# One attention head between half tiles, short divisors, projections by operand halves, an early first weight tile

## The chip, the cores and the metric

The kernel runs on one core of a Trainium2 chip. The metric is the device time of one execution in microseconds (us). TensorE (PE in the profile, PEld for its weight loads) does all matrix products, VectorE (DVE), ScalarE (ACT) and GpSimd (POOL) the rest, and SyncE (SP) issues the DMAs. The engines run their own instruction lists in order and meet at semaphores, which the program sets and waits for by hand.

## What is computed

Two blocks in a row on 256 tokens of width 1024: a gated delta-rule mixer, a forgetting attention, then a sliding-window attention beside a multiscale pooling, a merge, an output projection, and a dense evaluation of a routed expert layer with 16384 experts. The change touches the entrance of the first mixer and the middle of the second block:

```python
h = rmsnorm(x, norm_w[i]) * (1 + scale) + shift          # scale, shift from cond @ ada_w
proj = h @ w_in                                          # q k v z, then 16 columns b and 16 columns a
beta = sigmoid(b);  g = -exp(A_log) * softplus(a + dt_bias)
...
z = rmsnorm_2(h, ln_mix_g) @ w_in_2 + b_in_2             # 15 tiles of 256 columns: C_ORDER
q, k, v, pz, ga, gp = split(z)
y_a = sliding_window_attention(q, k, v, sinks) @ w_attn_up
cnt = minimum(t1, w);  pooled = (cj - lag) / cnt - pf    # windows w = 2, 4, 8, 16, t1 = 1..256
y_p = multiscale_pool(pz) @ w_pool_up
merged = sigmoid(ga) * y_a + sigmoid(gp) * y_p
h = h + merged @ w_o
```

## The kernel before

**Weight tiles.** Every large product runs over tiles of 1024 by 256 weights. A tile is loaded by one 1 MB DMA into one of four RAW slots (`load`), split by ACT into a rounded high part WHI (`hi`, L628 to L635) and by DVE into the rest WLO (`lo`, L1117 to L1121), each with two slots, and PE then makes three products for each of eight chunks of the operand: high by high, low by high, high by low. `columns_half` (L1803 to L1815) makes one half of the output columns' rows of a tile in 24 matmuls, `columns_tile` both halves in 48, `tokens_tile` (L1824 to L1835) the same number with the operand as the stationary side. The operand itself is split the same way: ACT writes XHI (`split_half`, L642), DVE XLO (`split_x`, L1131, and `split_low`, L1483), each in two halves of four chunks, and `x_halves` makes PE wait for a half when it comes to it (`x_split`). `tile_done` says that PE has finished a tile: `hi` waits for it before it overwrites the slot, two tiles on, and the eviction of the output bank waits for it too. `bank_free` says that one of the two output banks is evicted. Tiles are numbered through the whole program; T_AIN, T_CIN, T_PUP, T_AUP and T_WO are the first numbers of the first mixer's entrance, the second block's entrance, the pooling's up projection, the attention's up projection and the output projection.

**The beginning.** PE makes eight 256-column products of the modulation (L1861) while DVE turns each result into columns of MC by a product with the identity and a sum (L1188, L1190, loop n = 0 to 7). `norm(0)` on PE transposes x. When the eighth sum is there, DVE makes the scale and the shift (`modulation`), ACT writes H and XHI (L673, L642), DVE writes XLO. PE then multiplies H by the 32 columns of b and a (TWA, L1871, 16 matmuls that are two pieces each in the profile), and only then comes the first tile of T_AIN. `hi` and `lo` of that tile stand behind `norm(0)` on ACT and behind `split_x(0, H)` on DVE.

**The second block's entrance.** ACT evicts tile n of T_CIN with its bias (`project`, L937), and `hi` of tile n + 1 stands ahead of it. DVE has `lo` of the tiles one after another, with small work between the first ones: the divisors INV, first the smaller of t1 and w, then the reciprocal of all 256 columns for each of four windows (L1524, L1528), then four copies of v (L1533). POOL waits for these reciprocals (`inv_ready`) and makes the pooled sums, of which PE needs the last behind tile 8. Behind tile 11, whose columns are the first four heads' queries, PE has the logits of the first head (`logits(8)`, L2096 and L2097), then the whole tile 12. DVE has `lo` of tiles 4 to 13, then `queries_c(0)` (L1450, which the logits wait for), then `softmax(8)` (L1462 to L1479). ACT has `hi` of tile 13, the eviction of tile 12, and then the exponents (`exponents(8)`, L870). In eight rounds, one for a pair of heads, PE then transposes the probabilities (`turn`, L2106), makes the next logits, a half tile (or a tile with four chunks), and applies the probabilities to v (`apply`, L2116, L2117).

**The projections.** The attention's output feeds T_AUP (four tiles). DVE multiplies each result by its gate (L1572) and adds it to MG (L1574). When all four are added (`mg_done` 4) ACT splits MG (L642), DVE follows (L1131), and T_WO, four tiles by `tokens_tile`, starts with its first half.

## Time and profile before

| | us |
|---|---|
| median of 3 runs | 1847.93 |
| lowest, highest | 1843.86, 1848.80 |
| the profiled execution | 1848.02 |
| its span in the trace | 1846.3 |
| PE busy | 1708.7 (93%) |
| DVE, ACT, POOL busy | 1194.2, 900.3, 356.5 |

PE is busy for 93% of the span, but a busy PE is not always at full speed: the granted clock has two levels, 1.00 (2.4 GHz) and 0.50 (1.2 GHz), and it was 0.972 in the mean. So two things are to be read: where PE waits and for whom, and for how long the clock stands at 0.50 behind such a wait. In rows of the timeline the first number is the start in us from the beginning of the span, the second the duration, `xN` the number of merged instructions, and the bracket the idle time of the engine before the row with what ended it.

### The profile page before, as it was taken

How to read it: one execution, taken by the hardware profiler on the slowest of the kernel's cores; microseconds unless marked ns; L12 is line 12 of the kernel's file. 1: busy time of each engine (PE TensorE's matmuls, PEld its weight loads, DVE VectorE, ACT ScalarE, POOL GpSimd, SP SyncE). 2: the span in 40 equal slices, each digit the busy share in tenths (PEclk: the TensorE clock that was granted, in tenths of full speed). 3: DMA queues.
4: the chain of work that ended last, by engine and by line, in shares of the span. 5: the costliest groups of instructions: out<-in, count | busy, mean ns of one | idle time of the engine just before them, and what ended most of it. 6: DMA issues, size and time to landing. Idle time of an engine off the chain costs nothing.

```text
span 1846.3 us, 35420 instructions
## 1 busy us (share of the span) xinstructions
PE 1708.7 (93%) x11788; PEld 1572.8 (85%) x11788; DVE 1194.2 (65%) x2403; ACT 900.3 (49%) x1611; POOL 356.5 (19%) x225
## 2 busy tenths in 40 slices
PE   7899989999899986989889899999999989999998
PEld 6799788888799876988879899999999968888887
DVE  2686377776445655537633899968999865555554
ACT  1665523332335554445433344467777755555554
POOL 2000000000000000400000677776666420000000
PEclk9999999999899998999989899999999999999999
DMA  9555301010734333431553455555444356666664
GB/s 278 173 184 182 123 24 47 23 45 24 251 114 138 115 103 97 137 126 63 154 123 83 136 164 166 165 169 155 141 141 138 103 150 193 193 193 194 192 193 136
DMA packets 210746, 255.24 MB, mean 138 GB/s; under 512 B 14871, under 2 KB 192763, under 8 KB 210683
## 3 DMA queue, kind: packets, MB, share of 16 engines
q1 hardware_dynamic: 210683, 254.39, 45.6%
q8 instruction: 41, 0.67, 0.2%
q14 instruction: 22, 0.18, 0.0%
HBM read 253.29 MB, written 1.05 MB: 138 GB/s over the span
## 4 chain that ended last, share of the span: by engine, by line
PE 63%; issue 19%; POOL 8%; DVE 5%; ACT 3%; DMA 1%; SPq 1%; DVEq 0%; POOLq 0%; ACTq 0%
PE ps L2273 19%; PE ps L1815 13%; PE ps L2224 8%; POOL w_lo L618 7%; PE ps L2056 3%; PE ps L2249 3%; PE ps L1965 2%; PE ps L1954 2%; PE ps L1966 2%; PE ps L1861 2%; PE ps L1944 1%; PE ps L1835 1%; PE ps L1886 1%; PE ps L1905 1%; DMA raw<-in_u_experts 1%
## 5 line engine op out<-in xcount | busy, mean ns | idle before, releaser
L618 POOL TENSOR_TENSOR w_lo<-raw,w_hi 128x1024 fp32r<-128x1024 f32 x128 | 307.1, 2400 | 366.1 <-ACT w_hi L1009 365.5
L1815 PE MATMUL ps<-x_hi,w_hi 128*128 128x256 f32 x1104 | 319.8, 290 | 8.8 <-DVE w_lo L1121 5.7
L2224 PE MATMUL ps<-x_hi,w_hi 128*128 128x256 f32 x1024 | 297.4, 290 | 20.3 <-ACT arena L1014 12.4
L1815 PE MATMUL ps<-x_lo,w_hi 128*128 128x256 f32 x1104 | 315.4, 286 | 0.0
L1815 PE MATMUL ps<-x_hi,w_lo 128*128 128x256 f32 x1104 | 315.2, 286 | 0.0
L2224 PE MATMUL ps<-x_lo,w_hi 128*128 128x256 f32 x1024 | 290.7, 284 | 0.0
L2224 PE MATMUL ps<-x_hi,w_lo 128*128 128x256 f32 x1024 | 290.6, 284 | 0.0
L1779 DVE TENSOR_TENSOR w_lo<-raw,w_hi 128x1024 fp32r<-128x1024 f32 x124 | 152.0, 1226 | 143.8 <-ACT w_hi L1099 143.8
L1815 PEld LDWEIGHTS ps<-x_hi,w_hi 128*128 128x128 f32 x1104 | 215.1, 195 | 12.7 <-DVE w_lo L1121 6.4
L2224 PEld LDWEIGHTS ps<-x_hi,w_hi 128*128 128x128 f32 x1024 | 197.2, 193 | 24.6 <-issue 17.7
L1099 ACT ACTIVATE w_hi<-raw 128x1024 fp32r<-128x1024 f32 x124 | 131.6, 1061 | 172.9 <-PE ps L2273 172.9
L1815 PEld LDWEIGHTS ps<-x_lo,w_hi 128*128 128x128 f32 x1104 | 215.1, 195 | 0.5 <-issue 0.5
L1815 PEld LDWEIGHTS ps<-x_hi,w_lo 128*128 128x128 f32 x1104 | 214.9, 195 | 0.0
L2224 PEld LDWEIGHTS ps<-x_lo,w_hi 128*128 128x128 f32 x1024 | 197.5, 193 | 0.0
L2224 PEld LDWEIGHTS ps<-x_hi,w_lo 128*128 128x128 f32 x1024 | 197.2, 193 | 0.0
L1009 ACT ACTIVATE w_hi<-raw 128x1024 fp32r<-128x1024 f32 x128 | 134.8, 1053 | 123.9 <-DVE raw L1603 123.7
L1603 DVE STREAM_TRANSPOSE raw<-raw 128x1024 f32<-128x1024 f32 x128 | 158.4, 1238 | 22.2 <-DMA raw<-in_u_experts 17.0
L1121 DVE TENSOR_TENSOR w_lo<-arena,w_hi 128x2048 fp32r<-128x2048 f32 (+1 forms) x43 | 96.8, 2251 | 101.9 <-ACT w_hi L635 101.9
L2273 PE MATMUL ps<-w_hi,x_hi 128*128 128x512 f32 x512 | 158.7, 391 | 4.0 <-DVE x_lo L1774 4.0
L2273 PE MATMUL ps<-w_hi,x_lo 128*128 128x512 f32 x512 | 158.4, 391 | 0.0
L2273 PE MATMUL ps<-w_lo,x_hi 128*128 128x512 f32 x512 | 158.3, 390 | 0.0
L1121 DVE TENSOR_TENSOR w_lo<-raw,w_hi 128x2048 fp32r<-128x2048 f32 (+1 forms) x44 | 99.1, 2255 | 74.7 <-ACT w_hi L635 74.6
(336 smaller groups left out, 3235.3 us busy)
## 6 DMA issues: line engine op xcount, KB each, us to landing
raw<-in_u_experts SPq DMA_DIRECT2D x512, 128.0 KB, 2.5
raw<-in_v_experts SPq DMA_DIRECT2D x128, 512.0 KB, 4.3
arena<-in_ada_w SPq DMA_DIRECT2D x20, 1024.0 KB, 5.2
raw<-in_a_w_in SPq DMA_DIRECT2D x12, 1024.0 KB, 5.3
arena<-in_a_w_in SPq DMA_DIRECT2D x12, 1024.0 KB, 5.3
raw<-in_b_w_in SPq DMA_DIRECT2D x8, 1024.0 KB, 5.7
arena<-in_b_w_in SPq DMA_DIRECT2D x8, 1024.0 KB, 5.8
raw<-in_w_in SPq DMA_DIRECT2D x8, 1024.0 KB, 5.4
```

What stands on the lines that cost most here:

```text
L618: pool.tensor_tensor(UTL[e], UT[e % 2], UTH[e].bitcast(F32), ALU.subtract).then_inc(utl_ready, 1)
L1009: act.activation(UTH[e % 4], UT[e % 2], ACT.Copy).then_inc(uth_ready, 1)
L1099: act.activation(VH[u], VRAW[u], ACT.Copy).then_inc(high_ready, 1)
L1121: v.tensor_tensor(WLO[:, slot, 0:k, :], RAW[raw_slot(base, u)][:, 0:k, :], WHI[:, slot, 0:k, :].bitcast(F32), ALU.subtract).then_inc(lo_re ...
L1603: v.transpose(UT[s_].rearrange("p (k a j) -> p a k j", k=KC, a=4), URAW[s_].rearrange("p (a k i) -> p a k i", a=4, k=KC)).then_inc(ut_read ...
L1779: v.tensor_tensor(VL[u], VRAW[u], VH[u].bitcast(F32), ALU.subtract).then_inc(low_ready, 1)
L1815: ins = mm(o[:, b * S:b * S + S], w[:, slot, kk, b * P:b * P + P], xx[:, (kk + turn) % KC, :], start=(kk == 0 and n == 0), stop=(kk == k - ...
L1861: ins = mm(ps[u % 2][:, 0:TW], CONDR[:, kk, :], RAW[u][:, kk, :], start=(kk == 0), stop=(kk == KC - 1))
L2056: ins = mm(o, xx[:, kk, t * P:t * P + P], w[:, slot, kk, :], start=(kh == 0 and u % 2 == 0 and kk == 0 and n == 0), stop=(kh == 1 and kk = ...
L2224: ins = mm(ps[e % 2][:, 0:S], w[e % 4][:, kk * P:kk * P + P], xx[:, kk, :], start=(kk == 0 and n == 0), stop=(kk == KC - 1 and n == 2))
L2249: ins = mm(GB.rearrange("p (e t) -> p t e", t=4)[:, q, :], OHJ[:, c % 2, q, :], OHI[:, c % 2, q, :], start=True, stop=True, skip_group_che ...
L2273: ins = mm(ps[4 + 2 * t + h][:, :], g[:, u, t * P:t * P + P], w[u][:, 512 * h:512 * h + 512], start=False, stop=False, skip_group_check=True)
```

## The change

1. **First head among half tiles.** PE makes the first half of tile 12, the first head's logits, then the second half. DVE's `lo` of tile 13 moves behind `softmax(8)`, so that `queries_c(0)` follows `lo` of tile 12. ACT's eviction of tile 12 moves behind `exponents(8)`.
2. **Short divisors.** INV is filled with the constant 1/w by a memset, and the reciprocal is taken of the first w columns alone: 2, 4, 8 and 16 columns.
3. **Projections by operand halves.** The last T_AUP tile first makes chunks 4 to 7 for both output halves and signals `up_half`; ACT and DVE then split the first two merged tiles into chunks 4 to 7 of XHI and XLO while PE makes chunks 0 to 3. The first T_WO tile uses these chunks 4 to 7 first, for both token tiles, and chunks 0 to 3, with the last two merged tiles, after them. The other T_WO tiles take the chunks in the same turned order.
4. **The first T_AIN tile early.** `hi` of the tile stands behind ACT's `statistics(0)` and ahead of its wait for the modulation, `lo` ahead of the eighth pass of DVE's loop. PE has the tile ahead of the product for b and a. `hi` and `lo` of the third tile stand ahead of the tail. The product for b and a is one with 48 columns (b in 0 to 15, a in 32 to 47, the second layer's f weights between them) in place of two with 16, 8 matmuls in place of 16. For that TWA is loaded by two DMAs with rows of 64 B in place of one with 128 B, `rows_in` counts seven.

```diff
-            sp.dma_start(TWA, a_w_in[0, :, 6144:6176].rearrange("(k p) n -> p k n", p=P)).then_inc(rows_in, 16)
+            for g in range(2):
+                sp.dma_start(TWA[:, :, 32 * g:32 * g + 16],
+                             a_w_in[0, :, 6144 + 16 * g:6160 + 16 * g].rearrange("(k p) n -> p k n", p=P)).then_inc(rows_in, 16)
...
@@ scalar
                 statistics(r, eps)
+                if r == 0:
+                    hi(T_AIN, 0, 0)
...
-            for n in range(13):
+            for n in range(12):
                 hi(T_CIN, 0, n + 1)
                 project(n)
...
             act.wait_ge(c_pos, 4)
+            hi(T_CIN, 0, 13)
             exponents(8)
+            project(12)
...
+            act.wait_ge(mg_done, 2)
+            act.wait_ge(up_half, 1)
+            act.activation(XHI[:, 4:8, :], MG[:, 0:4, :], ACT.Copy).then_inc(xhi_ready, 1)
             act.wait_ge(mg_done, 4)
-            split_x(8, MG, 75)
+            act.wait_ge(tile_done, 75 + 2)
+            act.activation(XHI[:, 0:4, :], MG[:, 4:8, :], ACT.Copy).then_inc(xhi_ready, 1)
...
@@ vector
             for n in range(8):
+                if n == 7:
+                    lo(T_AIN, 0, 0)
                 v.wait_ge(raw_free, 4 + n + 1)
...
-                v.tensor_scalar(INV[:, j, :], T1, float(2 << j), None, ALU.min).then_inc(c_prep, 1)
+                v.memset(INV[:, j, :], 1.0 / (2 << j)).then_inc(c_prep, 1)
...
-                v.reciprocal(INV[:, j, :], INV[:, j, :]).then_inc(inv_ready, 1)
+                v.reciprocal(INV[:, j, 0:2 << j], T1[:, 0:2 << j]).then_inc(inv_ready, 1)
...
-            for n in range(4, 14):
+            for n in range(4, 13):
                 lo(T_CIN, 0, n)
             queries_c(0)
             softmax(8)
+            lo(T_CIN, 0, 13)
             queries_c(1)
...
                 lo(T_AUP, 0, u + 1)
+                if u == 3:
+                    split_low(8, 0, slice(4, 8), MG[:, 0:4, :])
                 product(T_AUP, 0, u)
...
@@ tensor
             norm(0)
-            pe.wait_ge(rows_in, 16 * 6)
+            x_round[0] = 0
+            columns_tile(T_AIN, 0, 0)
+            pe.wait_ge(rows_in, 16 * 7)
...
-            for j in range(2):
-                for kk in range(KC):
-                    ins = mm(ps[2][0:16, j * 256:j * 256 + 256], TWA[:, kk, 16 * j:16 * j + 16], H[:, kk, :],
-                             start=(kk == 0), stop=(kk == KC - 1))
+            for kk in range(KC):
+                ins = mm(ps[2][0:48, 0:256], TWA[:, kk, :], H[:, kk, :], start=(kk == 0), stop=(kk == KC - 1))
...
-                elif n == 11:
-                    pe.wait_ge(c_k, 1)
-                    pe.wait_ge(c_pos, 4)
-                    logits(8, cK[:, 0:S])
+            columns_half(T_CIN, 0, 12, 0)
+            pe.wait_ge(c_k, 1)
+            pe.wait_ge(c_pos, 4)
+            logits(8, cK[:, 0:S])
+            columns_half(T_CIN, 0, 12, 1)
...
+            for half in range(2):
+                pe.wait_ge(x_split, 17 + half)
+                for t in range(TT):
+                    for kk in range(4 * half, 4 * half + 4):
+                        for n, (xx, w) in enumerate(((XHI, WHI), (XLO, WHI), (XHI, WLO))):
+                            ins = mm(bank(T_WO, 0)[:, t * TW:t * TW + TW], xx[:, (kk + 4) % KC, t * P:t * P + P], w[:, slot, kk, :],
+                                     start=(kk == 0 and t == 0 and n == 0), stop=(kk == KC - 1 and n == 2), skip_group_check=True)
```

**The beginning, on DVE.** Before, with the two last passes of the modulation's loop (output banks ps0 and ps1), the scale and shift, the operand's low halves and the first two weight tiles' low parts:

```order
L1188 TENSOR_TENSOR arena<-ps0,small 128x256
L1190 TENSOR_REDUCE small<-arena 128x2
L1188 TENSOR_TENSOR arena<-ps1,small 128x256
L1190 TENSOR_REDUCE small<-arena 128x2
L1179 TENSOR_TENSOR small<-small 128x8
L1180 SCALAR_TENSOR_TENSOR small<-small 128x8
L1182 TENSOR_TENSOR small<-small 128x8
L1131 TENSOR_TENSOR x_lo<-arena,x_hi 128x1024 x2
L1121 TENSOR_TENSOR w_lo<-raw01,w_hi 128x2048 x2
```

The same place in the changed kernel:

```order
L1202 TENSOR_TENSOR arena<-ps0,small 128x256
L1204 TENSOR_REDUCE small<-arena 128x2
L1133 TENSOR_TENSOR w_lo<-raw01,w_hi 128x2048
L1202 TENSOR_TENSOR arena<-ps1,small 128x256
L1204 TENSOR_REDUCE small<-arena 128x2
L1191 TENSOR_TENSOR small<-small 128x8
L1192 SCALAR_TENSOR_TENSOR small<-small 128x8
L1194 TENSOR_TENSOR small<-small 128x8
L1143 TENSOR_TENSOR x_lo<-arena,x_hi 128x1024 x2
L1133 TENSOR_TENSOR w_lo<-raw01,w_hi 128x2048
L1133 TENSOR_TENSOR w_lo<-arena,w_hi 128x2048
```

The first tile's low part now stands ahead of the loop's last pass, and the third tile's low part, which reads the arena, has come up behind the second's.

**The second attention's beginning, on PE.** Before, the last matmuls of tile 11 (ps1), the first head's logits with their masks (ps2, ps4), and the first of tile 12 (ps0):

```order
L1815 MATMUL ps1<-x_hi,w_lo 128x256
L2096 MATMUL ps2<-arena 128x128
L2097 MATMUL ps2<-small 128x128
L2096 MATMUL ps2<-arena 128x256
L2097 MATMUL ps2<-small 128x256
L2096 MATMUL ps4<-arena 128x128
L2097 MATMUL ps4<-small 128x128
L2096 MATMUL ps4<-arena 128x256
L2097 MATMUL ps4<-small 128x256
L1815 MATMUL ps0<-x_hi,w_hi 128x256
```

In the changed kernel the rows on both sides of the logits are of tile 12:

```order
L1838 MATMUL ps0<-x_lo,w_hi 128x256
L1838 MATMUL ps0<-x_hi,w_lo 128x256
L2119 MATMUL ps2<-arena 128x128
L2120 MATMUL ps2<-small 128x128
L2119 MATMUL ps2<-arena 128x256
L2120 MATMUL ps2<-small 128x256
L2119 MATMUL ps4<-arena 128x128
L2120 MATMUL ps4<-small 128x128
L2119 MATMUL ps4<-arena 128x256
L2120 MATMUL ps4<-small 128x256
L1838 MATMUL ps0<-x_hi,w_hi 128x256
```

A half tile of 24 matmuls now stands between the end of tile 11 and the logits.

**From the last T_AUP tile to the first T_WO tile, on DVE.** Before, with the last two gated results (ps1, ps0) and the operand's low halves:

```order
L1572 TENSOR_TENSOR arena<-ps1,arena 128x512
L1574 TENSOR_TENSOR arena<-arena 128x512
L1121 TENSOR_TENSOR w_lo<-arena,w_hi 128x2048
L1572 TENSOR_TENSOR arena<-ps0,arena 128x512
L1574 TENSOR_TENSOR arena<-arena 128x512
L1131 TENSOR_TENSOR x_lo<-arena,x_hi 128x1024 x2
L1121 TENSOR_TENSOR w_lo<-raw01,w_hi 128x2048
L1157 TENSOR_TENSOR arena<-arena,ps1 128x2x256
```

The same place in the changed kernel:

```order
L1595 TENSOR_TENSOR arena<-ps1,arena 128x512
L1597 TENSOR_TENSOR arena<-arena 128x512
L1133 TENSOR_TENSOR w_lo<-arena,w_hi 128x2048
L1503 TENSOR_TENSOR x_lo<-arena,x_hi 128x1024
L1595 TENSOR_TENSOR arena<-ps0,arena 128x512
L1597 TENSOR_TENSOR arena<-arena 128x512
L1503 TENSOR_TENSOR x_lo<-arena,x_hi 128x1024
L1133 TENSOR_TENSOR w_lo<-raw01,w_hi 128x2048
L1169 TENSOR_TENSOR arena<-arena,ps1 128x2x256
```

One of the two operand halves has moved ahead of the last gated result.

## Rows read from the trace of the kernel before

**Rows 1.** Timeline, beginning; start, duration, engine, line, names, count, idle before

```profile
44.79 0.42 DVE L1188 TENSOR_TENSOR arena<-ps,small 128x256 f32<-128x256 f32 x1 [2.58 <-PE ps L1861]
49.24 1.23 DVE L1131 TENSOR_TENSOR x_lo<-arena,x_hi 128x1024 fp32r<-128x1024 f32 x1 [3.09 <-ACT x_hi L642]
52.15 1.23 DVE L1131 TENSOR_TENSOR x_lo<-arena,x_hi 128x1024 fp32r<-128x1024 f32 x1 [1.69 <-ACT x_hi L642]
...
51.18 0.58 PE L1867 MATMUL ps<-small 1*128 1x16 f32 x2 [4.67 <-ACT arena L673]
51.68 9.71 PE L1871 MATMUL ps<-arena,small 128*16 128x256 f32 x32
...
65.36 0.51 ACT L702 ACTIVATE arena<-arena,small 16x256 f32<-16x256 f32 x1
```

**Rows 2.** DMA: the first T_AIN tile's issue at 34.50, us to landing

```profile
raw<-in_a_w_in SPq DMA_DIRECT2D x1, 1024.0 KB, 6.7
```

**Rows 3.** DMA packets from 35.5 to 36.0 us, mostly TWA's

```profile
DMA packets 843, 0.11 MB, mean 211 GB/s; under 512 B 833, under 2 KB 843, under 8 KB 843
```

**Rows 4.** Windows: busy of PE, PEld, DVE, ACT, POOL, then PEclk, DMA share, GB/s

```profile
57.00:57.50 0.50, 0.50 (x3) 0.19 (x2) 0.50 (x1) 0.00 (x0) 0.00 (x0) 0.95 0.00 0
```

**Rows 5.** Timeline, ACT and DVE, around tile 4 of T_CIN

```profile
759.14 1.91 ACT L635 ACTIVATE w_hi<-raw 128x2048 fp32r<-128x2048 f32 x1
...
764.17 0.84 ACT L937 ACTIVATE arena<-ps,small 128x256 f32<-128x256 f32 x2 [1.82 <-PE ps L1815]
...
774.38 0.84 ACT L937 ACTIVATE arena<-ps,small 128x256 f32<-128x256 f32 x2 [7.58 <-PE ps L1815]
...
757.14 6.58 DVE L1528 RECIPROCAL arena<-arena 128x256 f32<-128x256 f32 x4
764.37 5.14 DVE L1121 TENSOR_TENSOR w_lo<-raw,w_hi 128x2048 fp32r<-128x2048 f32 x2
```

**Rows 6.** Timeline, ACT, DVE and PE, tile 11 to the second head's transposes

```profile
817.43 0.84 ACT L937 ACTIVATE arena<-ps,small 128x256 f32<-128x256 f32 x2 [2.71 <-PE ps L1815]
...
820.10 2.29 DVE L1121 TENSOR_TENSOR w_lo<-raw,w_hi 128x2048 fp32r<-128x2048 f32 x1 [3.05 <-ACT w_hi L635]
822.31 0.61 DVE L1450 TENSOR_SCALAR arena<-arena,small 128x256 f32<-128x256 f32 x2
...
823.07 0.77 PE L2096 MATMUL ps<-arena 128*128 128x128 f32 x2 [5.67 <-DVE arena L1450]
...
836.34 1.80 PE L2106 MATMUL ps<-small,arena 128*128 128x128 f32 x6 [2.99 <-DVE arena L1479]
...
844.56 0.60 PE L2116 MATMUL ps<-arena 128*128 128x256 f32 x2
...
845.87 0.82 PE L2106 MATMUL ps<-small,arena 128*128 128x128 f32 x6
```

**Rows 7.** Timeline, PE, first and last piece of a later head's logits

```profile
880.23 0.39 PE L2096 MATMUL ps<-arena 128*128 128x128 f32 x2
...
881.87 0.27 PE L2097 MATMUL ps<-small 128*128 128x256 bf16 x1
```

**Rows 8.** Timeline, DVE, first and last step of a later head's softmax

```profile
854.20 0.62 DVE L1462 TENSOR_REDUCE small<-ps 128x1 f32<-128x128 f32 x2 [1.11 <-PE ps L2097]
...
857.75 0.55 DVE L1479 TENSOR_SCALAR arena<-arena,small 128x128 f32<-128x128 f32 x2
```

**Rows 9.** Windows of PE: busy, granted clock, DMA share, GB/s

```profile
835.00:836.00 1.00, 0.00 (x0) 0.65 0.00 0
```

**Rows 10.** Timeline, DVE, last T_AUP tile and first T_WO tiles

```profile
917.74 0.69 DVE L1572 TENSOR_TENSOR arena<-ps,arena 128x512 f32<-128x512 f32 x1 [1.46 <-PE ps L1815]
...
920.35 2.36 DVE L1131 TENSOR_TENSOR x_lo<-arena,x_hi 128x1024 fp32r<-128x1024 f32 x2 [1.19 <-ACT x_hi L642]
...
930.27 0.69 DVE L1157 TENSOR_TENSOR arena<-arena,ps 128x512 f32<-128x512 f32 x1 [4.96 <-PE ps L1835]
...
936.03 0.69 DVE L1157 TENSOR_TENSOR arena<-arena,ps 128x512 f32<-128x512 f32 x1 [1.46 <-PE ps L1835]
```

86 lines of the change are left out of this document (54 added, 32 removed).

## The prediction

> **What bounds the kernel now.** I read the waits of TensorE first. It is busy nearly throughout, so a microsecond taken from any other engine counts only where PE waits for it. Then I read the timeline around each long wait, to see which instruction ended it and what stood ahead of that instruction in its queue, and last the windows with the granted clock, because behind each long wait the clock stands at 0.50 for some microseconds and PE's own work takes twice as long. The change addresses four places. (a) At the beginning PE idles 4.67 us for the normed input and then spends 9.71 us on the product for b and a, of which the first 5.4 us are at half clock: the clock was back at 57.05 [rows 1, 4]. (b) Tile 4 of the second block's entrance: the evictions of tiles 3 and 4 start 10.21 us apart, against 5.76 between two tiles that wait for nothing [rows 5, 10]. (c) The first head of the second attention: PE idles 5.67 us for its queries and 2.99 us for its softmax [rows 6]. (d) Between the last up tile and the first output tile the evictions are 12.53 us apart, again against 5.76 [rows 10].
>
> A tile of 48 matmuls is 5.76 us at full clock, 0.12 a matmul, a half tile 2.88, and at half clock the double is an upper bound. All four gains lie on PE's path, and what follows each is timed from PE's progress (weight loads wait for `lo_ready`, which moves along), so I add them and take nothing off further down.
>
> **(b) Short divisors.** The four reciprocals of 256 columns take 6.58 us, and `lo` of tile 4 stands behind them: it starts at 764.37, though its high part was there at 759.14 + 1.91 = 761.05, and tile 3 is done at 764.13 [rows 5]. With 2 to 16 columns, 30 in place of 1024, the four cost a fraction of that; even at 1 us together the copies are done before 761.05, `lo` runs from there to about 763.4 (763.7 at the 2.57 that it takes beside POOL), and PE waits for nothing. The memsets take the place of four instructions of like size, with more than 1 us of slack behind them. What goes is the wait of 2.7 us and the half clock that it caused: 10.21 - 5.76 = **4.45 us**. POOL gets its divisors earlier too; its results are needed only behind tile 8. If `lo` of tile 4 came late by a POOL operation, 0.5 us of this would be lost: 3.9 to 4.5.
>
> **(c) The first head.** Times are those of the old trace. Tile 11 is done at 817.38. PE goes on with the first half of tile 12, whose low part is ready, to 820.3. DVE has nothing ahead of the queries but the eviction of tile 11 (817.43 + 0.84), so they are ready at 818.9, and the logits start at 820.3 with no wait. At full clock they take 1.76 us, from 880.23 to 0.12 behind 881.87 [rows 7]. Second half of tile 12 to 824.9. The softmax of a head takes 4.1 us from its first reduction to its last product (854.20 to 858.30) [rows 8]; it starts 1.1 us into the logits, at 821.4, and ends at 825.5, so the wait of 2.99 us becomes one of about 0.6, and the six transposes end at 826.1. Now the new wait: `lo` of tile 13 (2.2) and the next queries (0.6) stand behind the softmax on DVE, and the next logits need the queries: 825.5 + 2.8 = 828.3. PE waits 2.2 us; nobody but PE waits for that. Then logits 1.76, a half tile 2.88 and the application 1.31 (844.56 to 845.87 [rows 6]) give 834.3 for the next transposes, which stood at 845.87: 11.6 us. I take off 0.7, an estimate: ACT's and DVE's split of tile 14 (1.9 and 2.3) now comes later against PE than before and delays the third head's reductions.
>
> How the clock takes the new wait is open. It was granted full until 0.3 us into the window from 835 to 836 (0.65 in its mean), so it fell about 2 us into the wait that had begun at 833.35 [rows 6, 9]; The new wait of 2.2 us with 0.6 just ahead of it is near that one, so I assume that it falls, and comes back within 3.5 to 6 us of work. That costs half of 3.4 at the least, 3 at the most, and some is covered by the softmax: I take 1.6. Term: 11.6 - 0.7 - 1.6 = **9.3 us**; ends 7.5 and 11.6.
>
> **(d) Operand halves.** The first merged half (chunks 4 to 7) can be split when the last up tile, which runs from 911.94 to 917.70, is half done, at 914.8. `hi` (1.9) and `lo` (2.3) of the output tile follow the tile before and keep DVE until 916.3; with 1.23 for the operand's low part it ends at 917.5, just ahead of the last up tile's end at 917.70. So the output tile starts there, without the wait for 921.7. Its first 24 matmuls end at 920.6. The second half is ready as the old first one was, 920.35 + 1.23 = 921.6 [rows 10]. PE waits 1.1 us and ends the tile at 921.7 + 2.9 = 924.6, against 930.23 before. Next late would be `lo` of the second output tile: ACT splits it from 920.2 to 922.1, DVE from 922.2 to 924.5, a tie. Term: **5.6 us**, with 4.5 if the tie is lost and 6.0 as the upper end.
>
> **(a) The early tile.** The first tile lands 6.7 us after its issue at 34.50, so at 41.2 [rows 2]. Ahead of it in the queue there are now 1024 more rows of 64 B. 833 such small packets went in half a microsecond [rows 3], so 1024 take 0.6, and with the issue I take 0.7: landing 41.9. ACT's high part (1.92) is ready at 43.8, DVE's low part (2.25) at 46.1, and the loop's last product, which ran at 44.79, stands behind it: everything from there to XLO is 1.3 us later. That wait is the price of this part, and ACT, PE and all behind them pay it. The ends are 0.6 (no slower landing at all) and 2.5 (packets twice as slow).
>
> The Trainium skill's page DMA: Bandwidth & Descriptors, section Why small descriptors are slow, says a packet costs a cycle per 32 B and about 3 more. By it two rows of 64 B cost 10 cycles where one of 128 B costs 7, so TWA would add not 0.6 but about 0.26 us, and this term would be 0.4 larger. In the trace the packet rate hardly depended on the size (833 of mostly 128 B in one half microsecond), so I keep 0.7.
>
> PE then starts the tile at 50.6 + 1.3 = 51.9, at half clock. Its first 12 matmuls (0.24 at most, 0.214 as the pieces of the old row show) end at 54.5, the second operand half is there at 53.5 + 1.3 = 54.8. As before the clock returns 5.9 us after the restart, at 57.8: 14 matmuls by then, 22 more at 0.12: done at 60.5. The product for b and a has 16 pieces in place of 32; the old ones took 0.22 each once the clock was back, so 3.5, with the sinks' 0.2 it ends at 64.2. The second tile ends at 70.0. Before, two tiles followed 61.39 and ended at 72.9. Term: **2.9 us**, ends 1.5 and 4.3. The evacuation of the first bank stands behind ACT's tail, which took 4.5 us (61.39 to 65.87 [rows 1]) and takes until 68.7, with the bank's copy 69.3: 0.7 ahead of need.
>
> **Sum.** 2.9 + 4.45 + 9.3 + 5.6 = 22.25 us. The profiled execution took 1848.02, 0.1 above the median, so the forecast is 1848.02 - 22.25 = 1825.8 us. The runs of before spread by 5 us, which the range has to hold too.
>
> **Rivals.**
>
> *The clock holds in (c), or the softmax runs beside more.* For it: the wait is shorter than the one behind which the clock is seen to fall [rows 9]. It gives 1.6 to 2.3 us more, and with the upper ends of (a) and (d) 1820 to 1821.
>
> *The early tile costs what it brings.* DVE's low part in the loop holds back the whole norm. If the tile lands after 43.5, the loss there is over 3 us and (a) brings about 1: 1828; with (d)'s tie lost too 1829 to 1830. Against it: nothing else of size is in the DMA queue ahead of the tile.
>
> *(c) brings half.* If the second head's chain (exponents, `lo` of tile 13, queries) is longer than the rows say by the eviction of tile 12, which ACT now does between, and the clock is low through two rounds, the term is 5: 1830.
>
> *The other side: the clock does not come back in the attention.* A later round has some 6.7 us of PE work at full clock (0.7 + 1.76 + 2.88 + 1.31). If the new wait of 2.2 us let the clock fall and each following softmax wait kept it low, seven rounds would take up to 6.7 us more each, 47 in all, less the 22: 1873. It decides at whether PE is kept busy through the round behind the wait. Before, it was, after a longer idle time: by 845.87 the six transposes took 0.82 us, where behind the wait they took 1.80 [rows 6]. The Trainium skill's page TensorE: Matmul & The Clock Gate, section HAM oscillation, describes such a loop, whose bursts are short against its waits and which runs at the low clock in every round. In the rounds here the transposes of the next head follow the application at once (845.87, with no idle time [rows 6]), so the trace so far speaks against it.
>
> *It does not do what it says.* That would be so if PE found the halves unready everywhere: the order shows each moved instruction in its place, so this is left to single terms.
>
> **How the numbers follow.** The forecast case, all four terms within their ends, 1821.5 to 1829: 0.76. More than that, under 1821.5: 0.09. Early tile or first head worth half, 1829 to 1835: 0.11. Between 1835 and 1842.4: 0.02. The clock stays low, or another mishap that leaves no gain: 0.02. A measurement of this kernel can tell about 0.3%, 5.5 us, from no change. Faster by more than that (under 1842.4) is then 0.98, within it 0.01, slower 0.01. The range 1820 to 1831.5 leaves out some 0.05 below and 0.1 above.
>
> **What would show it.** (b): evictions of tiles 3 and 4 are 5.8 us apart, and no wait for `w_lo` there. (c): no wait ahead of the first logits, one of about 2.2 us ahead of the second, and the time from the eviction of tile 11 to the second head's transposes is 17 to 19 us, where it was 28.4. (d): a wait of about 1.1 us in the middle of the first output tile, and evictions 6.9 us apart, where they were 12.5. (a): DVE's last product of the loop 1.3 us later than 44.79, the second tile done at about 70. I would be wrong if the clock were low for longer than 7 us at a time anywhere in the attention, or if a new wait stood behind these places on another engine.

## The result, and the profile after

The changed kernel takes 1821.32 us (median of 6 runs, 1816.2 to 1824.96) where the kernel before took 1845.71 beside it (6 runs, 1843.1 to 1848.8): ratio 0.9866, with a 95% interval from 0.9844 to 0.9889. The forecast was 1825.8 in 1820 to 1831.5, so the median lies inside the range, 4.5 us under the forecast and just below the forecast case (1821.5 to 1829, chance 0.76), in the stretch that was given 0.09. It is no run's time: three runs lie at 1816.2 to 1818.64 and three at 1823.99 to 1824.96. The profiled execution took 1823.99 (span 1822.1), 24.0 less than the profiled one of before, where the sum said 22.25. One of the ten runs of the operand halves alone, below, took 2825.75 us at a mean granted clock of 0.556 and is left out of its median and ratio.

All places are read between the same two landmarks in both traces:

| place and landmarks, us | before | after | gain | forecast |
|---|---|---|---|---|
| (a) second T_AIN tile done (ACT's next high part) | 73.20 | 70.27 | 2.93 | 2.9 |
| (b) evictions of tiles 3 and 4 apart | 10.21 | 5.80 | 4.41 | 4.45 |
| (c) eviction of tile 11 to the second head's transposes | 28.44 | 19.57 | 8.87 | 10.0 |
| from these transposes to the last T_AUP eviction | 71.87 | 71.84 | 0.03 | -0.7 |
| (d) last T_AUP eviction to first T_WO eviction | 12.53 | 7.07 | 5.46 | 5.6 |
| from the second T_AIN tile to the eviction of tile 3 | 690.97 | 689.18 | 1.8 | 0 |
| from the fourth T_WO eviction to the end | 898.75 | 898.05 | 0.7 | 0 |

The forecast's 9.3 for (c) is 11.6 less 1.6 for the clock, which lie between these landmarks, and less 0.7, which lies behind them.

**The beginning** (timeline of after: start us, duration us, engine, line, names, count, idle before; it answers to [rows 1]):

```profile
41.41 0.43 DVE L1202 TENSOR_TENSOR arena<-ps,small 128x256 f32<-128x256 f32 x1 [2.57 <-PE ps L1884]
...
41.86 1.91 ACT L638 ACTIVATE w_hi<-raw 128x2048 fp32r<-128x2048 f32 x1 [24.61 <-DMA raw<-in_a_w_in]
...
43.80 2.29 DVE L1133 TENSOR_TENSOR w_lo<-raw,w_hi 128x2048 fp32r<-128x2048 f32 x1 [1.51 <-ACT w_hi L638]
46.01 0.42 DVE L1202 TENSOR_TENSOR arena<-ps,small 128x256 f32<-128x256 f32 x1
...
50.44 1.22 DVE L1143 TENSOR_TENSOR x_lo<-arena,x_hi 128x1024 fp32r<-128x1024 f32 x1 [3.08 <-ACT x_hi L645]
...
60.56 3.65 PE L1894 MATMUL ps<-arena,small 128*48 128x256 f32 x16
...
70.27 1.92 ACT L638 ACTIVATE w_hi<-arena 128x2048 fp32r<-128x2048 f32 x1 [0.17 <-PE ps L1838]
```

The same two landmarks before, the loop's seventh product and ACT's high part behind the second tile:

```profile
41.34 0.42 DVE L1188 TENSOR_TENSOR arena<-ps,small 128x256 f32<-128x256 f32 x1 [2.58 <-PE ps L1861]
...
73.20 1.92 ACT L635 ACTIVATE w_hi<-arena 128x2048 fp32r<-128x2048 f32 x1 [2.42 <-PE ps L1815]
```

The tile lands at 41.86 (41.9 was said), DVE's low part ends as the loop's last product starts, at 46.01 (46.1), and that product is 1.2 later than before. The price is plain to see: the first operand half starts at 50.44, where it stood at 49.24.

**Tile 4 of the second block** (timeline of after, DVE and ACT; it answers to [rows 5]):

```profile
752.43 0.44 DVE L1548 RECIPROCAL arena<-arena 128x2 f32<-128x2 f32 x4
...
756.37 2.78 DVE L1133 TENSOR_TENSOR w_lo<-raw,w_hi 128x2048 fp32r<-128x2048 f32 x1 [2.77 <-ACT w_hi L638]
...
759.45 0.84 ACT L943 ACTIVATE arena<-ps,small 128x256 f32<-128x256 f32 x2 [1.82 <-PE ps L1838]
...
765.25 0.84 ACT L943 ACTIVATE arena<-ps,small 128x256 f32<-128x256 f32 x2 [3.16 <-PE ps L1838]
```

The four reciprocals take 0.44 us together where they took 6.58. DVE now idles 2.77 us ahead of the low part and waits for ACT's high part; before, the high part was there and the low part stood behind the reciprocals.

**The first head** (timeline of after, ACT, DVE and PE; it answers to [rows 6]):

```profile
808.30 0.84 ACT L943 ACTIVATE arena<-ps,small 128x256 f32<-128x256 f32 x2 [2.71 <-PE ps L1838]
...
815.59 0.55 DVE L1499 TENSOR_SCALAR arena<-arena,small 128x128 f32<-128x128 f32 x2
816.06 2.28 DVE L1133 TENSOR_TENSOR w_lo<-raw,w_hi 128x2048 fp32r<-128x2048 f32 x1
818.26 0.61 DVE L1470 TENSOR_SCALAR arena<-arena,small 128x256 f32<-128x256 f32 x2
...
810.98 0.39 PE L2119 MATMUL ps<-arena 128*128 128x128 f32 x2
...
815.60 1.14 PE L2129 MATMUL ps<-small,arena 128*128 128x128 f32 x6
...
818.92 0.79 PE L2119 MATMUL ps<-arena 128*128 128x128 f32 x2 [2.18 <-DVE arena L1470]
...
827.87 0.82 PE L2129 MATMUL ps<-small,arena 128*128 128x128 f32 x6
```

The first logits (810.98) wait for nothing. The new wait stands where it was forecast, ahead of the second head's logits, and is 2.18 us long: softmax, then `lo` of tile 13, then the queries. The windows of after there (us; busy of PE, PEld, DVE, ACT, POOL; granted clock; DMA) show the clock go to its half level, 1.2 GHz, within that wait and come back 6.8 us of half clock later:

```profile
818.00:819.00 1.00, 0.08 (x1) 0.08 (x1) 0.87 (x3) 0.00 (x0) 0.00 (x0) 0.68 0.00 0
...
825.00:826.00 1.00, 1.00 (x10) 1.00 (x9) 0.93 (x5) 1.00 (x1) 0.00 (x0) 0.90 0.00 0
```

**Up and out projection** (timeline of after, DVE and PE, then its window; it answers to [rows 10]):

```profile
899.71 0.69 DVE L1595 TENSOR_TENSOR arena<-ps,arena 128x512 f32<-128x512 f32 x1 [0.32 <-PE ps L2211]
...
902.32 1.23 DVE L1503 TENSOR_TENSOR x_lo<-arena,x_hi 128x1024 fp32r<-128x1024 f32 x1 [1.20 <-ACT x_hi L994]
...
906.78 0.69 DVE L1169 TENSOR_TENSOR arena<-arena,ps 128x512 f32<-128x512 f32 x1 [0.44 <-PE ps L2222]
...
903.60 0.39 PE L2222 MATMUL ps<-w_hi,x_hi 128*128 128x256 f32 x1 [0.96 <-DVE x_lo L1503]
```

```profile
900.00:904.00 4.00, 3.04 (x25) 2.83 (x25) 2.31 (x3) 2.85 (x2) 0.00 (x0) 1.00 1.11 230
```

One wait of 0.96 in the middle of the tile (1.1 was said), at full clock throughout.

**What the sum did not have.** Between (a) and (b) no numbered part of the change removes work or a wait, and yet 1.8 us went there. The wait at the second block's entrance is the same to the hundredth; before, then after:

```profile
731.82 3.67 PE L1843 MATMUL ps<-small,arena 128*128 128x128 f32 x16 [11.30 <-DVE arena L1142]
```

```profile
728.68 3.67 PE L1866 MATMUL ps<-small,arena 128*128 128x128 f32 x16 [11.30 <-DVE arena L1154]
```

What differs is how long the clock is low around it: the windows of before show 0.52 over 21 us, those of after 0.55 over 14 us and then 0.95:

```profile
722.00:743.00 21.00, 9.52 (x43) 9.15 (x44) 9.13 (x8) 12.43 (x23) 0.74 (x2) 0.52 0.20 64
```

```profile
718.00:732.00 14.00, 3.32 (x16) 3.27 (x16) 4.70 (x6) 7.49 (x17) 0.74 (x2) 0.55 0.29 94
732.00:743.00 11.00, 8.55 (x68) 8.02 (x67) 5.92 (x7) 6.83 (x10) 0.00 (x0) 0.95 0.22 70
```

Adding up (1 - granted clock) x 2 x width over windows of 2 us gives 20.5 us at half clock there before and 13.7 after, and over the whole span 102.7 before and 78.7 after. All times at half clock below are worked out so. Of the 24 us fewer, 3.4 lie behind the wait of (b), 6.8 at (c), 6.8 at (d) and 6.8 at this entrance.

The other traces bear this place out. The wait is 11.29 or 11.30 in all 14. The stretch from the second T_AIN tile to the eviction of tile 3 takes 690.8 to 691.0 us in the three with 20.5 us at half clock at the entrance (before, c_head_alone, three_moves) and 689.0 to 689.5 in the nine with 13.7, whether the change is in them or not.

The 0.7 behind the output projection is another matter: there both traces have the same half clock (10.2, 10.2 and 6.8 us at three places, and the clock low from about 4 us before the end). Six traces with this pattern take 897.8 to 898.8 us for that stretch, so 0.7 is inside what that stretch varies by, and its cause is open.

### The profile page after: what moved, and what is told of

It reads as the page before. It is cut to its first block, busy times and chain, and to the rows that moved or that the text cites. A ratio compares the mean times of both kernels' runs of the same rounds, so it can differ in the third digit from the quotient of the medians.

```text
span 1822.1 us, 35333 instructions
## 1 busy us (share of the span) xinstructions
PE 1696.4 (93%) x11772; PEld 1565.1 (86%) x11772; DVE 1187.0 (65%) x2403; ACT 900.1 (49%) x1611; POOL 357.0 (20%) x225
## 4 chain that ended last, share of the span: by engine, by line
PE 63%; issue 19%; POOL 8%; DVE 5%; ACT 3%; DMA 1%; SPq 1%; DVEq 0%; POOLq 0%; ACTq 0%
PE ps L2318 19%; PE ps L1838 13%; PE ps L2269 9%; POOL w_lo L621 7%; PE ps L2079 3%; PE ps L2294 3%; PE ps L1988 2%; PE ps L1977 2%; PE ps L1989 2%; PE ps L1967 2%; PE ps L1858 1%; PE ps L1909 1%; PE ps L1884 1%; PE ps L1928 1%; PE ps L2119 1%
## 5 line engine op out<-in xcount | busy, mean ns | idle before, releaser
L2269 PE MATMUL ps<-x_hi,w_hi 128*128 128x256 f32 x1024 | 297.5, 291 | 19.7 <-ACT arena L1026 11.8
L1838 PEld LDWEIGHTS ps<-x_hi,w_hi 128*128 128x128 f32 x1088 | 211.0, 194 | 16.3 <-issue 9.1
L2269 PEld LDWEIGHTS ps<-x_hi,w_hi 128*128 128x128 f32 x1024 | 197.1, 192 | 24.1 <-issue 17.3
L1838 PEld LDWEIGHTS ps<-x_lo,w_hi 128*128 128x128 f32 x1088 | 211.1, 194 | 0.5 <-issue 0.5
L1838 PEld LDWEIGHTS ps<-x_hi,w_lo 128*128 128x128 f32 x1088 | 210.9, 194 | 0.0
L2269 PEld LDWEIGHTS ps<-x_lo,w_hi 128*128 128x128 f32 x1024 | 197.4, 193 | 0.0
L2269 PEld LDWEIGHTS ps<-x_hi,w_lo 128*128 128x128 f32 x1024 | 197.1, 193 | 0.0
```

Source lines behind the costliest of these rows:

```text
L1838: ins = mm(o[:, b * S:b * S + S], w[:, slot, kk, b * P:b * P + P], xx[:, (kk + turn) % KC, :], start=(kk == 0 and n == 0), stop=(kk == k - ...
L2269: ins = mm(ps[e % 2][:, 0:S], w[e % 4][:, kk * P:kk * P + P], xx[:, kk, :], start=(kk == 0 and n == 0), stop=(kk == KC - 1 and n == 2))
```

## Experiments

Each kernel is the one before with one part, or the changed one with one to three edits. "Beside it" is the kernel before in the same series.

### One part alone

Four kernels, each the one before with the lines of one numbered part of the change and nothing else: part 4 (T_AIN's `hi`, `lo` and `columns_tile` early, TWA by two DMAs, 48 columns), part 2, part 1 (tile 12 by halves around `logits(8)`, `lo` of tile 13 behind `softmax(8)`) and part 3 (`up_half`, chunks 4 to 7 first). Their diffs are pieces of the one shown; that of part 2 is

```diff
-                v.tensor_scalar(INV[:, j, :], T1, float(2 << j), None, ALU.min).then_inc(c_prep, 1)
+                v.memset(INV[:, j, :], 1.0 / (2 << j)).then_inc(c_prep, 1)
-                v.reciprocal(INV[:, j, :], INV[:, j, :]).then_inc(inv_ready, 1)
+                v.reciprocal(INV[:, j, 0:2 << j], T1[:, 0:2 << j]).then_inc(inv_ready, 1)
```

Part 4, the early tile. 

> The kernel before with the early first weight tile and the 48-column product alone. Theory: the terms stand at separate places and add, so this is worth what the landmark shows in the full change, 2.9 us (second tile done at about 70.3 us in place of 73.2), and the median falls by 3 us. A rival, that most of the full change's 24 us comes from PE's clock everywhere and not from the four places, expects a fall of more than 6 us or none here, with the mean granted clock moved.

Part 2, the divisors. 

> The kernel before with the short divisors alone. Theory of separate places: the evictions of tiles 3 and 4 of the second block's entrance are 5.8 us apart in place of 10.2, the median falls by 4.4 us, and the tiles behind show no new wait. The rival (clock everywhere) expects another sum than 4.4, by more than 3 us.

Part 1, the first head. 

> The kernel before with the first head between the two halves of tile 12 alone. Theory: from the eviction of tile 11 to the second head's transposes 19.6 us in place of 28.4, a fall of 8.9 us; the wait for the second head's queries is 2.2 us, and the clock falls behind it as in the full change. If the clock holds in this run (its fall depends on where the wait lies), 10.5 to 11 us.

Part 3, the operand halves. 

> The kernel before with the up and output projections by operand halves alone. Theory: the evictions of the last up tile and the first output tile are 7.1 us apart in place of 12.5, the clock stays at 1.00 through the wait of 1 us in the middle of the output tile, and the median falls by 5.5 us.

| part alone | median (range, runs), beside 1843.95 | ratio [95%] | at its own landmarks |
|---|---|---|---|
| (a) | 1839.79 (1837.67 to 1845.31, 10) | 0.9973 [0.9958, 0.9987] | loop's seventh product to second tile 28.56, was 31.86 |
| (b) | 1841.01 (1839.68 to 1845.53, 10) | 0.9983 [0.9971, 0.9994] | 5.82, was 10.21 |
| (c) | 1837.09 (1832.43 to 1838.6, 5) | 0.9948 [0.9927, 0.9969] | 18.32, was 28.44 |
| (d) | 1837.49 (1835.56 to 1841.59, 9) | 0.9961 [0.9947, 0.9974] | 7.07, was 12.53 |

The medians fall by 4.2, 2.9, 6.9 and 6.5, 20.4 together, and the whole change's by 20 (its second series, below) to 24 (its first). Expected were 3, 4.4, 8.9 and 5.5, so (b) and (c) fell short by 1.5 and 2, and (a) and (d) went beyond by about 1. Each interval is 2 to 4 us wide to either side, so the medians agree with parts that add but can't prove it. The rival of the first expectation (most of the 24 us is the clock everywhere, so that the early tile alone brings over 6 us or nothing, with its mean clock moved) isn't borne out: 4.2 us, at mean clocks of 0.972 to 0.977 as in the kernel before. The landmarks decide better: alone the parts gain 3.3, 4.4, 10.1 and 5.5 there, against 3.0, 4.4, 8.9 and 5.5 in the whole, so none is hidden behind another. In (c) alone the second wait has less half clock behind it (3.4 us instead of 6.8). For (a) the seventh product is the base, because the run of (a) alone is 0.5 us ahead before that landmark.

The trace of (d) alone holds a clean price for the old wait in (b), since that part is undone here and the clock happened to hold (timeline, then a window):

```profile
764.43 0.39 PE L1821 MATMUL ps<-x_hi,w_hi 128*128 128x256 f32 x1 [2.70 <-DVE w_lo L1125]
```

```profile
766.00:768.00 2.00, 2.00 (x19) 2.00 (x18) 1.11 (x1) 0.00 (x0) 2.00 (x3) 1.00 0.98 322
```

The evictions of tiles 3 and 4 are 8.73 apart there and 10.21 in before. So of (b)'s gain 2.9 (8.73 - 5.82) is the wait, and 1.5 is what the 3.4 us of half clock behind it cost.

### The two new waits taken away

On the changed kernel, the second head's queries ahead of the low part:

```diff
             softmax(8)
-            lo(T_CIN, 0, 13)
             queries_c(1)
+            lo(T_CIN, 0, 13)
```

> The changed kernel, with the second head's queries ahead of the low part of tile 13 on DVE. Theory: the wait of 2.2 us ahead of the second head's logits and the half clock behind it (from 818.7 to 825.1) are both of this order. With it turned, PE waits less than 0.5 us there, the clock stays at 1.00, PE then waits about 0.5 us for the low part of tile 13, and the second head's transposes start 4 to 5 us earlier than 827.87; 1 to 2 us of it are given back in the next round, where tile 14's split delays the third head's reductions. Net 3 us. Rival: the gap is not what lets the clock fall, or the softmax chain takes its place: less than 1 us.

Measured 1817.79 (1816.98 to 1818.06, 4 runs) beside 1843.96: 0.9848 [0.9828, 0.9868]. Its timeline, DVE then PE, and a window:

```profile
815.08 0.61 DVE L1470 TENSOR_SCALAR arena<-arena,small 128x256 f32<-128x256 f32 x2
815.61 2.28 DVE L1133 TENSOR_TENSOR w_lo<-raw,w_hi 128x2048 fp32r<-128x2048 f32 x1
...
815.75 0.49 PE L2119 MATMUL ps<-arena 128*128 128x128 f32 x2
...
822.22 0.82 PE L2129 MATMUL ps<-small,arena 128*128 128x128 f32 x6
```

```profile
817.00:818.00 1.00, 0.81 (x6) 0.40 (x4) 1.00 (x2) 0.00 (x0) 0.00 (x0) 1.00 0.00 0
```

The second logits follow the transposes with no idle time, and the clock stays full. From the eviction of tile 11 (807.32) to the second head's transposes it is 14.90, 4.67 less than in the changed kernel. A part is given back (1 to 2 us were expected): from there to the last T_AUP eviction it takes 72.45 where it took 71.84, because one later round takes 7.18 instead of 6.59. Net, from the eviction of tile 11 to the last T_AUP eviction, it is 87.35 against 91.41, 4.1 less (3 was expected).

The early tile's low part out of the loop:

```diff
             for n in range(8):
-                if n == 7:
-                    lo(T_AIN, 0, 0)
...
             modulation(0, MC[:, 0:8], MC[:, 8:16], 0)
+            lo(T_AIN, 0, 0)
             split_x(0, H)
```

> The changed kernel, with the first weight tile's low part behind the scale and shift on DVE, ahead of the operand's low half. Theory: the prediction's price of 1.3 us for the early tile is DVE's low part in the loop. DVE is idle for 3.1 us behind the modulation, and the low part takes 2.3, so the loop's last product is back at about 44.8, everything behind it 1.2 us earlier than in the changed kernel, second tile done at about 69.1. Rival (the norm is late for another reason, the DMA or ACT): no gain.

Measured 1821.64 (1821.47 to 1824.71, 4 runs), 0.9875 [0.9853, 0.9897]. In its trace the eighth product follows the seventh by 3.46, in the changed kernel by 4.60, so the low part inside the loop costs 1.1:

```profile
40.31 0.42 DVE L1200 TENSOR_TENSOR arena<-ps,small 128x256 f32<-128x256 f32 x1 [2.57 <-PE ps L1883]
...
43.77 0.42 DVE L1200 TENSOR_TENSOR arena<-ps,small 128x256 f32<-128x256 f32 x1 [2.58 <-PE ps L1883]
...
45.04 2.29 DVE L1133 TENSOR_TENSOR w_lo<-raw,w_hi 128x2048 fp32r<-128x2048 f32 x1
```

From the seventh product to the second tile's end it is 27.74 here and 28.86 in the changed kernel. The expected 1.2 is met, and the rival of no gain is out. The median doesn't show that 1.1: its trace has 17.1 us at half clock behind the T_WO tiles where the changed kernel's has 10.2, and 2.4 us more from the fourth T_WO eviction to the end. It tells something else too. The wait of (c) is in it, 2.18 us as before, and the clock held:

```profile
816.80 0.49 PE L2118 MATMUL ps<-arena 128*128 128x128 f32 x2 [2.18 <-DVE arena L1469]
```

```profile
816.00:817.00 1.00, 0.20 (x1) 0.20 (x2) 0.75 (x3) 0.00 (x0) 0.00 (x0) 1.00 0.00 0
```

Landmark to landmark it is 16.67 (806.17 to 822.84). The changed kernel's 19.57 with 6.8 us at half clock, and 18.32 with 3.4 us in (c) alone, then price the half clock: 2.9 and 1.65. From the eviction of tile 11 to the last T_AUP eviction this trace takes 88.67, so the queries moved first (87.35) are worth 1.3 us where the clock holds behind the wait, and 4.1 where it stands low for 6.8 us.

Both of these edits together (both_moves):

> The changed kernel with both moves: the second head's queries ahead of the low part of tile 13, and the first weight tile's low part behind the scale and shift. The gains add: 3 + 1.2, so some 4 us below the changed kernel, 28.5 below the kernel before.

Measured 1820.76 (1816.11 to 1822.41, 4 runs), 0.9868 [0.9845, 0.989]. The beginning (27.79) and the first head (14.91) are as in the two single ones; the fastest run is the fastest of all, but two of four are at 1822.4. So the moves add locally, but the median is 23.2 below the kernel before and not the expected 28.5, and not better than the better move alone.

### What the tail's loads cost

The changed kernel with TWA and its product as before:

```diff
-            for g in range(2):
-                sp.dma_start(TWA[:, :, 32 * g:32 * g + 16],
-                             a_w_in[0, :, 6144 + 16 * g:6160 + 16 * g].rearrange("(k p) n -> p k n", p=P)).then_inc(rows_in, 16)
+            sp.dma_start(TWA, a_w_in[0, :, 6144:6176].rearrange("(k p) n -> p k n", p=P)).then_inc(rows_in, 16)
...
-            for kk in range(KC):
-                ins = mm(ps[2][0:48, 0:256], TWA[:, kk, :], H[:, kk, :], start=(kk == 0), stop=(kk == KC - 1))
+            for j in range(2):
+                for kk in range(KC):
+                    ins = mm(ps[2][0:16, j * 256:j * 256 + 256], TWA[:, kk, 16 * j:16 * j + 16], H[:, kk, :],
+                             start=(kk == 0), stop=(kk == KC - 1))
```

> The changed kernel with the product for b and a as before: one DMA with rows of 128 B, two products of 16 columns. Theory: the first tile lands 0.7 us earlier (41.2 in place of 41.86), so the operand's low half and the tile start 0.7 earlier, and PE takes 3.5 us more for the product: second tile done at about 73.0, 2.8 us later than the changed kernel, so that the early tile without the smaller product gains next to nothing. By the Trainium skill's page DMA: Bandwidth & Descriptors the landing would differ by about 0.3 us.

Measured 1827.71 (1824.08 to 1827.9, 4 runs), 0.9896 [0.9873, 0.9919]. The trace: the tile lands 0.47 ahead of the loop's seventh product (next fence), where it lands 0.45 behind it in the changed kernel. So 1024 rows more in the queue cost 0.9 us, not the 0.7 of the forecast. The landing itself varies: 0.36 to 1.15 behind that product in the seven traces with the changed kernel's small loads, 0.1 to 0.5 ahead in the five with the old ones; between the means it is 0.9 too. The product for b and a takes 7.08 instead of 3.65.

To the second tile's end it is 30.28 from the seventh product against 28.86, 1.4 more, half of the 2.8 expected. That is no clean price of the loads and the product: here the clock stood low for 3.4 us at the first tile, in the changed kernel for 6.8, and the first tile takes 1.1 less for it (7.33 from its start to the row behind it, against 8.43). With the same clock it would be about 2.5 (an estimate, 1.4 + 1.1), close to what was expected.

```profile
40.98 1.91 ACT L636 ACTIVATE w_hi<-raw 128x2048 fp32r<-128x2048 f32 x1 [23.71 <-DMA raw<-in_a_w_in]
...
41.45 0.42 DVE L1200 TENSOR_TENSOR arena<-ps,small 128x256 f32<-128x256 f32 x1 [2.58 <-PE ps L1882]
```

TWA's two DMAs and TWB's (taken from ahead of the loop) behind the second T_AIN tile's:

```diff
             for u in range(4):
                 load(T_AIN, 0, u, a_w_in[0], TW * u)
+                if u == 1:
+                    for g in range(2):
+                        sp.dma_start(TWA[:, :, 32 * g:32 * g + 16],
+                                     a_w_in[0, :, 6144 + 16 * g:6160 + 16 * g].rearrange("(k p) n -> p k n", p=P)).then_inc(rows_in, 16)
+                    sp.dma_start(TWB, b_w_in[0, :, 4096:4112].rearrange("(k p) n -> p k n", p=P)).then_inc(rows_in, 16)
```

> The changed kernel, with the three loads of small rows (3072 packets) issued behind the first two weight tiles. Theory: small packets cost about 0.95 us per 1024, so the first tile lands 2 to 2.8 us earlier against the loop (before the loop's seventh product, not 0.4 us behind it), and the low part in the loop delays nothing: the eighth product follows the seventh by 3.45 us in place of 4.6, and the second tile is done 1.1 us earlier. If the page's price held (0.26 us per extra 1024), the landing would move by less than 1 us.

Measured 1822.87 (1822.12 to 1823.53, 4 runs) beside 1843.97, 0.988 [0.9861, 0.9898]. Landing against the seventh product:

```profile
38.66 1.91 ACT L638 ACTIVATE w_hi<-raw 128x2048 fp32r<-128x2048 f32 x1 [21.48 <-DMA raw<-in_a_w_in]
...
40.27 0.42 DVE L1202 TENSOR_TENSOR arena<-ps,small 128x256 f32<-128x256 f32 x1 [2.58 <-PE ps L1884]
40.73 0.42 DVE L1204 TENSOR_REDUCE small<-arena 128x2 f32<-128x256 f32 x1
41.06 2.28 DVE L1133 TENSOR_TENSOR w_lo<-raw,w_hi 128x2048 fp32r<-128x2048 f32 x1
```

It is 1.61 ahead, 2.06 earlier than in the changed kernel (2 to 2.8 were expected), for 3072 rows of 64 B moved behind it: 0.69 us per 1024. The low part now fits into the loop's idle time (41.06), the last product isn't held up (3.45 behind the seventh), and the beginning takes 27.70. That removes the price of (a), and the median again can't tell it: this trace too has 17.1 us at half clock behind the T_WO tiles.

The queries first, the low part out of the loop and the small loads later, together (three_moves):

> The changed kernel with the queries first, the low part behind the modulation, and the small loads later: 1.1 us from the beginning and, from the second attention, 1.2 us where the clock holds in the changed kernel and 4 where it falls for 6.8 us. Median 2 to 5 us below the changed kernel's of the same call. The small loads add nothing to the other move. Rival, that the clock's phase hides such steps: no difference of the medians.

Measured 1821.15 (1816.3 to 1823.08, 5 runs), 0.9858 [0.9838, 0.9878]. Beginning 28.07, first head 14.91, but 20.5 us at half clock at the second block's entrance and 17.1 behind the T_WO tiles in its profiled run. The median is 2.8 below that of the changed kernel in the same series (1823.9, next), inside the expected 2 to 5, but three of its five runs are at 1821 to 1823 and the ratios' intervals overlap. Which version is best stays open.

### How far a profile of one execution speaks for the kernel

The changed kernel once more, with no edit (changed_again):

> The changed kernel once more, beside the next two on one chip. Theory: its times spread over some 8 us with the mean granted clock (0.977 to 0.984) and not with any of the four places; median near 1820, and the median of the kernel before near 1844.

Measured 1823.9 (1823.66 to 1824.7, 4 runs), 0.9885 [0.9867, 0.9903]; first head 19.57, (b) 5.80, (d) 7.08, as in its first profile. The profile repeats. The expected spread of 8 us about 1820 did not come: all four runs lie at the lower mean clock (0.978), and the median is 2.6 above the first series'.

And queries_first once more, with no further edit (queries_first_again):

> The kernel of queries_first once more, to see whether its four runs (1817.0 to 1818.1, clock 0.982) are its own level or one phase of the clock. Theory of phases: the times come in groups some 5 us apart, with mean clocks 0.977 to 0.978 and 0.982 to 0.984, and both turn up here too, the slower at 1821 to 1823; the median of many is 2 to 4 us below the changed kernel's. Rival, that the move itself keeps the clock up in every run: all runs at 1817 to 1818.

Measured 1817.87 (1817.79 to 1818.28, 4 runs) beside 1847.39, 0.9852 [0.9832, 0.9872]. I had expected a second group of slower runs, as the kernel before has one; none came. So the rival, that this version is at the higher clock in every run, stands in these two series (8 of 8 runs between 1817.0 and 1818.3). Why isn't settled: both_moves and three_moves contain the same edit and did have slower runs, and the series ran on different chips, which no run separates from the edit.

## Why the prediction was right, point by point

**The view.** That PE is the bound and only its waits count held: each of the four parts gained alone, and at the landmarks the gains added. The order of reading (waits, then what ended them, then the clock behind them) gave three terms within 0.2 us and the fourth, (c), within 0.5 by two errors.

**(a), 2.9, measured 2.93.** The steps came out within 0.3 (landing 41.9 and 41.86; last product 46.1 and 46.01; b and a done 64.2 and 64.15; second tile 70.0, which at the table's landmark is 70.3, and 70.27), but for the clock, which was back at 57.2 and not at 57.8. The price inside it, 1.3, is 1.1 to 1.2 by the two kernels that take it away. The landing was right by luck. The sum held the issue at 34.50 and added 0.7 to the 6.7 behind it; in fact SyncE issued the tile at 36.07, since the TWA and TWB loads ahead of it kept SyncE for 1.14 and 1.62 us where they had taken 0.42 and 0.83, and it landed 5.8 after that. And I priced 1024 rows at 0.7 from a half microsecond that held 833 packets [rows 3]; the runs give 0.9 for 1024 rows split in two, 0.69 per 1024 for rows moved away. That bears out the row's rate against the rule weighed there (the one row, mostly of 128 B, could not show that rows of 64 B go at the same rate; the runs do, about 1500 per us against its 1690): by the Trainium skill's page DMA: Bandwidth & Descriptors, section Why small descriptors are slow (HBM only), the splitting would have cost about 0.26, by the prediction's estimate, and the measured 0.9 is over three times that.

**(b), 4.45, measured 4.41.** Right, and now its two parts are known: 2.9 wait and 1.5 clock.

**(c), 9.3, measured 8.87, by two errors that nearly cancel.** The gross gain was right: 28.44 - 16.67 = 11.8 with the clock held, where 11.6 was said; the wait of 2.2 was 2.18. The deduction of 0.7 for tile 14's later split was wrong: from the second head's transposes to the last T_AUP eviction it takes 71.84 where it took 71.87. It grows only where the second head comes earlier: 72.00 with the clock held (low_part_behind_modulation), 72.45 with the queries first. The clock's term was mis-sized: 1.6 is what 3.4 us at half clock cost (1.65), but the profiled run had 6.8, and that costs 2.9, inside the upper end of 3 that was stated. 11.8 - 2.9 = 8.9. By the sign that the prediction set for itself, 17 to 19 us between the landmarks, the measured 19.57 is outside, by the same 1.3 of clock.

**(d), 5.6, measured 5.46.** The wait was 0.96 for 1.1, and the tie at the second output tile was not lost: the evictions from there are 5.75 apart (906.78, 912.53).

**What was missing: the clock where nothing was changed.** The four terms measure 21.7, the profiled executions differ by 24.2 in span. Of the rest, 1.8 is half clock at the second block's entrance, which the change doesn't touch, and 0.7 is unexplained, as said above. The rest of the 4.5 us between forecast and median comes from the base. The profiled run of before, 1848.02, belongs to the slower of two groups that the kernel's runs form, and I took it for the median, which three runs then put at 1847.93 and six at 1845.71. The runs of one kernel, by their mean granted clock:

| kernel | runs at the higher mean clock | runs at the lower |
|---|---|---|
| before | 0.975 to 0.977: 1841.9 to 1844.4 | 0.972 to 0.974: 1847.0 to 1849.6 |
| changed | 0.982 to 0.984: 1816.2 to 1818.6 | 0.977 to 0.978: 1823.7 to 1825.0 |
| queries_first | 0.982 to 0.983: 1817.0 to 1818.3 | none in 8 |

By the medians of the groups, lower to lower the change gives 1848 to 1824, 24 us; higher to higher 1843.5 to 1818.3, 25. The forecast of 1825.8 was one for the lower group, and there it missed by 2. That the measured 1821.32 lies inside the range owes something to luck: it is the middle between two groups, and the higher one alone (1816.2 to 1818.64) lies below the range's 1820. A forecast should have said that the median can fall into either.

One place where the groups of the changed kernels differ can be seen. The three profiled runs at 0.982 and 0.983 (queries_first, queries_first_again, both_moves) have 3.4 us at half clock near 1460 us, in the expert layer, and take 896.3 to 896.7 us from the fourth T_WO eviction to the end; the other profiled runs with all four parts have 6.8 there, and the changed kernel's two take 897.8 and 898.05. None of these edits touches that layer, and no profile of the changed kernel itself in its higher group was taken. So this shows where, not why.

**The rivals.** The clock that never comes back did not occur: it was full again by 826 in the changed kernel, and in the rounds behind it the six transposes take 0.82 (827.87, 834.46). (c) did not bring half, and its clock was low in one round only. The early tile did not land after 43.5 in any trace (42.3 at the latest, queries_first_again). The cheaper case of (c), the clock holding, is real, but in other executions (low_part_behind_modulation, small_loads_later: 16.67).

**A better version.** `queries_c(1)` ahead of `lo(T_CIN, 0, 13)` is one line moved. Against the kernel before it has 0.9848 and 0.9852, and it is below the changed kernel by its medians (1817.8; changed 1821.3 and 1823.9, in other series). In its best run the changed kernel is as fast (1816.2). At the landmarks the move is worth 1.3 us where the clock holds behind the wait and 4.1 where it is low for 6.8 us. The rest of the 3.5 to 6 us between the medians is the group that the runs fall in, 1.4 of it in the profiled runs behind the output projection, and that the move brings that about isn't shown.

## What to carry to other kernels

When two instructions wait on one engine, put the short one that the bounding engine needs next ahead of the long one that it needs later: 0.6 us of queries behind 2.3 us of low part made a wait of 2.18 us, with up to 2.9 us lost to the half clock behind it. Price a wait as its length plus what the clock costs, with two or three values for the latter, and check in which group of runs the profiled execution lies before its time is used as the base. An edit of 1 us that is plain between two landmarks of the trace may be invisible in medians whose runs spread by 6.

## What the runs showed of the hardware

**One wait, three outcomes of the clock.** The same wait of 2.18 us at the same place had 0 (low_part_behind_modulation, small_loads_later), 3.4 (c_head_alone, old_tail) and 6.8 us (the changed kernel, both times) at half clock behind it, one of 2.70 us 3.4 (the kernel before) or 0 (d_operand_halves_alone), and an unchanged wait of 11.30 had 10.2 to 20.5 us around it. The runs don't show what sets which. The Trainium skill's page TensorE: Matmul & The Clock Gate, Part 1, says that the number of matmuls that a kernel runs at the low clock at its start varies between runs. The traces here show the same of waits in the middle of a kernel, and the runs form groups by their mean clock, some 5 us (before) and 6 us (changed) apart.

**A one-column copy that takes 2.25 us.** POOL's copy of a single column takes 0.19 us, but as long as DVE's low part when that runs (timeline of after, POOL):

```profile
754.60 0.19 POOL L611 COPY arena<-arena 128x1 f32<-128x1 f32 x1 [29.40 <-ACT arena L943]
...
756.26 0.74 POOL L615 TENSOR_TENSOR arena<-arena 128x256 f32<-128x256 f32 x1
756.94 2.25 POOL L611 COPY arena<-arena 128x1 f32<-128x1 f32 x1
...
759.82 0.19 POOL L611 COPY arena<-arena 128x2 f32<-128x2 f32 x1
```

It ends at 759.19, DVE's low part (756.37, 2.78, shown above) at 759.15; the next one, 762.15 for 2.30, ends with DVE's next low part (762.12, 2.29) likewise. DVE's own instruction takes 2.78 instead of 2.29 when POOL's work overlaps its start. Nothing waited for POOL here, but these copies of one column could not have been costed from their size beside a DVE instruction that reads two operands. The profile's spans on POOL are rough; the agreement of the ends in both cases is what speaks for the reading.
